# Gate slabs and output projection of the first block as unsplit float32 matmuls

## The reference

```
def mixer_ab(x, ...):
    z = rms_norm(x, norm) @ w_in
    z_gate, z_rec, z_pool = z[..., :1024], z[..., 1024:2048], z[..., 2048:]
    xr = causal_dwconv(z_rec, conv_w, conv_b)
    y_a = gelu(z_gate) * rg_lru(xr, w_gx, b_gx, w_ga, b_ga, lam)
    y_b = multi_scale_pool(z_pool, w_pool, b_pool, pool_scale)
    return concatenate([y_a, y_b], -1) @ w_out      # 1536 -> 1024
x = x + mixer_ab(x, ...)
x = x + cross_attn(x, mem, ...)                     # q from x; k, v from mem
x = x + conv_ffn(x, ...)
```

## Time and profile before

| what | value |
|---|---|
| median of 3 runs | 1840.26 us (1838.64 to 1845.79) |
| the profiled execution's own time | 1839.95 us |
| its span, first to last instruction | 1838.2 us |
| mean granted TensorE clock | 0.958 of full speed |
| busy: PE, PEld, DVE, ACT, POOL | 93%, 75%, 47%, 36%, 29% of the span |
| chain that ended last | PE 38%, issue 31%, DVE 23%, ACT 6% |

### The profile page before, as it was taken

One profiled execution on the slowest core, in us unless ns is written; L12 is line 12 of the kernel. 1 busy time (PEld: TensorE's weight loads), 2 busy tenths in 40 slices (PEclk: granted clock), 3 DMA queues, 4 the chain that ended last, 5 costly groups with the idle time before them and its releaser, 6 DMA issues.

```text
span 1838.2 us, 31174 instructions
## 1 busy us (share of the span) xinstructions
PE 1713.1 (93%) x11954; PEld 1383.8 (75%) x11954; DVE 861.1 (47%) x1409; ACT 657.1 (36%) x1127; POOL 536.1 (29%) x329
## 2 busy tenths in 40 slices
PE   7998989999999998999998999987889999989886
PEld 7887979999998797999998998877844444333333
DVE  2787447888772353588785335765411011000002
ACT  2383444444455544434433334654311111111101
POOL 0443424555467431355552443221100000000000
PEclk9999999999899989999997999998889999999997
DMA  7464523555554442355551554333779999999992
GB/s 268 153 206 152 179 92 125 185 180 177 166 167 132 161 161 82 126 186 180 174 187 40 171 185 151 101 104 125 280 307 409 409 409 409 409 410 409 409 409 91
DMA packets 108973, 398.79 MB, mean 217 GB/s; under 512 B 12097, under 2 KB 12353, under 8 KB 108481
## 3 DMA queue, kind: packets, MB, share of 16 engines
q1 hardware_dynamic: 107856, 393.26, 58.9%
q10 hardware_dynamic: 1008, 4.08, 0.6%
HBM read 396.25 MB, written 1.05 MB: 216 GB/s over the span
## 4 chain that ended last, share of the span: by engine, by line
PE 38%; issue 31%; DVE 23%; ACT 6%; POOL 1%; DVEq 1%; DMA 0%; ACTq 0%; SPq 0%; POOLq 0%
DVE wl L1154 6%; DVE cf L1455 5%; PE pw L1864 5%; PE pw L1865 5%; PE pw L1866 5%; ACT wh L636 4%; PE pw L2114 4%; DVE hid L1471 3%; PE acc L1864 3%; PE acc L1865 3%; PE acc L1866 3%; DVE cf L1458 3%; PE acc L1873 3%; PE acc L1983 2%; DVE gpad L1449 1%
## 5 line engine op out<-in xcount | busy, mean ns | idle before, releaser
L1030 POOL TENSOR_TENSOR wl<-raw,wh 128x1024 fp32r<-128x1024 f32 x165 | 402.7, 2441 | 516.0 <-ACT wh L636 515.3
L636 ACT ACTIVATE wh<-raw 128x1024 fp32r<-128x1024 f32 x330 | 342.2, 1053 | 257.6 <-PE pw L1866 151.3
L1864 PE MATMUL pw<-ah,wh 128*128 128x256 f32 x1416 | 410.2, 290 | 4.0 <-DVE gt L1604 4.0
L1865 PE MATMUL pw<-ah,wl 128*128 128x256 f32 x1416 | 406.0, 287 | 0.0
L1866 PE MATMUL pw<-al,wh 128*128 128x256 f32 x1416 | 405.7, 287 | 0.0
L1154 DVE TENSOR_TENSOR wl<-raw,wh 128x1024 fp32r<-128x1024 f32 x165 | 214.6, 1301 | 235.9 <-ACT wh L636 235.8
L1864 PEld LDWEIGHTS pw<-ah,wh 128*128 128x128 f32 x1416 | 277.6, 196 | 8.2 <-issue 6.8
L1865 PEld LDWEIGHTS pw<-ah,wl 128*128 128x128 f32 x1416 | 277.4, 196 | 0.0
L1866 PEld LDWEIGHTS pw<-al,wh 128*128 128x128 f32 x1416 | 277.2, 196 | 0.0
L1864 PE MATMUL acc<-yh,wh 128*128 128x256 f32 x832 | 245.5, 295 | 23.7 <-POOL yl L1099 5.4
L1865 PE MATMUL acc<-yh,wl 128*128 128x256 f32 x832 | 242.2, 291 | 0.0
(11 more groups left out here) (296 smaller groups left out, 2561.9 us busy)
## 6 DMA issues: line engine op xcount, KB each, us to landing
raw<-in_stream SPq DMA_DIRECT2D x506, 512.0 KB, 3.7
ring_w<-in_stream SPq DMA_DIRECT2D x96, 512.0 KB, 12.8
ring_y<-in_stream SPq DMA_DIRECT2D x72, 512.0 KB, 13.9
ring_m<-in_stream SPq DMA_DIRECT2D x48, 512.0 KB, 12.9
ring_h<-in_stream SPq DMA_DIRECT2D x24, 512.0 KB, 13.7
mem_t<-in_mem ACTq DMA_DIRECT2D x2, 1024.0 KB, 9.4
x_res<-in_x SPq DMA_DIRECT2D x2, 512.0 KB, 6.3
out<-x_res SPq DMA_DIRECT2D x1, 1024.0 KB, 3.9
```

Of the source, the lines that this page charges most:

```text
L636: A.done(act.activation(wh[:, s.base % SPLIT, :], raw[:, slot_of(s.base), :], ACT.Copy), w_hi)
L1030: G.done(pool.tensor_tensor(wl[:, s.base % SPLIT, :], raw[:, slot_of(s.base), :], wh[:, s.base % SPLIT, :].bitcast(F32), ALU.subtract), w_ ...
L1864: pe.matmul(dst, wh[:, s.base % SPLIT, w], hi, start=start, stop=False, **kw)
L1865: pe.matmul(dst, wl[:, s.base % SPLIT, w], hi, start=False, stop=False, **kw)
```

## The change

The gate slabs of `gk` and all slabs of `about` are no longer split. TensorE multiplies them as in `abin`, one float32 matmul a tile out of `raw`, with `xr` and `z` themselves as activations (`tile1`); the keys and values stay split. So the casts and subtractions into `yh` and `yl` of this block go, with their semaphores: `xr_hi`, `xr_lo`, `pooled_hi`, `pooled_lo`, `yb_hi`, `yb_lo`, `ya_hi`, `ya_lo`. In the diff, `split` is ScalarE's. Splits are numbered anew by `split_no`, and VectorE and POOL alternate by that number. The first four query slabs' splits now wait for slab s-16 instead of s-4. ScalarE waits once for all four pooled groups before the gates, since their low-part subtraction, which ordered the temporaries before, is gone. SP's loads wait for the end of an unsplit slab.

```diff
 def unsplit(s):
-    return s < S0["gk"] or S0["cw"] <= s < S0["cw"] + CW
+    if S0["gk"] <= s < S0["v0"]:
+        return (s - S0["gk"]) % 3 == 0
+    return s < S0["gk"] or S0["about"] <= s < S0["q0"] or S0["cw"] <= s < S0["cw"] + CW
...
 def split_no(s):
-    return s - S0["gk"] - (0 if s < S0["cw"] else CW)
+    if s < S0["v0"]:
+        return s - S0["gk"] - (s - S0["gk"] + 2) // 3
+    if s < S0["about"]:
+        return s - S0["gk"] - 4
+    return s - S0["gk"] - 4 - 12 - (0 if s < S0["cw"] else CW)
...
             def split(s):
...
                 if S0["v1"] <= s.base < S0["v1"] + SPLIT:
                     wait_slab(act, s + -(SPLIT + CW))
+                elif S0["q0"] <= s.base < S0["q0"] + SPLIT:
+                    wait_slab(act, s + -(SPLIT + 12))
...
+            act.wait_ge(S("pooled"), 4)
...
-                wait_emptied(act, USE0["gk"] + 5 * n + 2)
-                A.done(act.activation(yh[:, 8 + n, :], z[:, 16 + n, :], ACT.Copy), S("yb_hi"))
...
             for n in range(8):
                 if n < 7:
                     split(At(S0["v0"] + n + 1 + AHEAD))
-                act.wait_ge(S("ya_ready"), n + 1)
-                A.done(act.activation(yh[:, n, :], xr[:, n, :], ACT.Copy), S("ya_hi"))
...
-                if n:
-                    ya_lo(n - 1)
                 if n == 4:
                     v0_out(0)
-            ya_lo(7)
             v0_out(1)
...
+            def tile1(dst, s, n, src, start, stop, **kw):
+                return pe.matmul(dst, raw[:, slot_of(s.base), n * P:n * P + P], src, start=start, stop=stop, **kw)
...
-                wait_split(pe, s)
+                wait_raw(pe, s)
                 for e in range(2):
                     h = 2 * n + e
                     wait_emptied(pe, u + e - 4)
-                    pe.wait_ge(S("xr_lo"), h + 1)
+                    pe.wait_ge(S("xr_ready"), h + 1)
                     for g in range(2):
-                        last = tile3(pw[(u + e) % 4][:, g * T:g * T + T], s, 2 * e + g, yh[:, h, :], yl[:, h, :],
-                                     True, True)
+                        last = tile1(pw[(u + e) % 4][:, g * T:g * T + T], s, 2 * e + g, xr[:, h, :], True, True)
...
-            row_phase("about", [8, 9, 10, 11, 0, 1, 2, 3, 4, 5, 6, 7],
-                      lambda k: pe.wait_ge(S("yb_lo"), k - 7) if k >= 8 else pe.wait_ge(S("ya_lo"), k + 1), "mem")
+            for n in range(12):
+                s = At(S0["about"] + n)
+                wait_raw(pe, s)
+                if n < 4:
+                    wait_emptied(pe, USE0["gk"] + 5 * n + 2)
+                else:
+                    pe.wait_ge(S("ya_ready"), n - 3)
+                for c in range(KC):
+                    last = tile1(acc_of(c), s, c, z[:, 16 + n, :] if n < 4 else xr[:, n - 4, :],
+                                 n == 0 and c % 2 == 0, n == 11, skip_group_check=True)
```

More of the change, by code:

```diff
@@ L435, in wait_split @@
         def wait_split(eng, s):
-            if s.base % 2 == 0:
+            if split_no(s.base) % 2 == 0:
                 eng.wait_ge(w_lo_v, s.of(lambda n: split_no(n) // 2 + 1))
@@ L552, in _ @@
                 sp.dma_start(x[:, 4 * half:4 * half + 4, :], x_in[:, 4 * half:4 * half + 4, :]).then_inc(x_landed[half], 16)
-            for s in range(3 * RAW):
+            for s in range(6 * RAW):
                 load(At(s))
-            early, late = S0["cw"] // RAW - 2, -(-(S0["cw"] + CW) // RAW) + 1
+            early, late = S0["cw"] // RAW - 5, -(-(S0["cw"] + CW) // RAW) + 1
             with sp.Fori(0, early) as i:
                 for j in range(RAW):
-                    load(At(3 * RAW + j, RAW, i))
-            for s in range((early + 3) * RAW, late * RAW):
+                    load(At(6 * RAW + j, RAW, i))
+            for s in range((early + 6) * RAW, late * RAW):
                 load(At(s))
@@ L686, in _ @@
                                           scale=col("a_conv_w", h * CONV_A + CONV_A - 1)), S("xr_first"))
-                if n - 1 in TAP_AT:
-                    h = TAP_AT.index(n - 1)
-                    act.wait_ge(S("xr_ready"), h + 1)
-                    A.done(act.activation(yh[:, h, :], xr[:, h, :], ACT.Copy), S("xr_hi"))
                 if 8 <= n < 12:
@@ L693, in _ @@
                     mem_hi(0, 2 * n - 15)
-                if n in (9, 12, 15, 18):
-                    g = n // 3 - 3
-                    act.wait_ge(S("pooled"), g + 1)
-                    A.done(act.activation(yh[:, 8 + g, :], z[:, 16 + g, :], ACT.Copy), S("pooled_hi"))
                 if n >= 14:
@@ L1065, in _ @@
                     G.done(pool.tensor_tensor(z[:, 16 + g, :], src, z[:, 16 + g, :], ALU.subtract), S("pooled"))
-                if n in (10, 13, 16, 19):
-                    g = (n - 10) // 3
-                    pool.wait_ge(S("pooled_hi"), g + 1)
-                    G.done(pool.tensor_tensor(yl[:, 8 + g, :], z[:, 16 + g, :], yh[:, 8 + g, :].bitcast(F32),
-                                              ALU.subtract), S("pooled_lo"))
             splits(S0["gk"], 12)
@@ L1274, in xr_taps @@
                                                     ALU.mult, ALU.add), S("xr_ready") if k == CONV_A - 1 else None)
-            def xr_lo(h):
-                dve.wait_ge(S("xr_hi"), h + 1)
-                V.done(dve.tensor_tensor(yl[:, h, :], xr[:, h, :], yh[:, h, :].bitcast(F32), ALU.subtract),
-                       S("xr_lo"))
             def slab_out(s, u, dst):
@@ L1335, in _ @@
                 split(At(gate_slab(n) + AHEAD))
-                if n == 0:
-                    xr_lo(7)
                 u = USE0["gk"] + 5 * n
@@ L2146, in _ @@
             pe.wait_ge(S("v0_out"), TT)
-            row_phase("about", [8, 9, 10, 11, 0, 1, 2, 3, 4, 5, 6, 7],
-                      lambda k: pe.wait_ge(S("yb_lo"), k - 7) if k >= 8 else pe.wait_ge(S("ya_lo"), k + 1), "mem")
+            for n in range(12):
[8 more added lines that the diff above has]
+                                 n == 0 and c % 2 == 0, n == 11, skip_group_check=True)
+                    if n == 11 and c < KC - 1:
+                        last.then_inc(acc_full, 1)
+                last.then_inc(slab_done, 1)
             def spread_hook(name):
```

18 lines of the change are left out of this document (4 added, 14 removed).

## The result

The changed kernel takes **1824.0 us**, median of 5 runs (1816.49 to 1827.48), against 1839.43 us of the kernel before in the same comparison (5 runs, 1834.89 to 1845.79): ratio 0.9914, 95% interval 0.9886 to 0.9942. That is faster by 15.4 us and by more than 0.5%. Its profiled execution took 1825.4 us with a span of 1823.6, against 1839.95 and 1838.2. The prediction was 1831.1 us with a range from 1827.0; the measured time lies 3.0 us under the range.

A forecast was written before the change was run, and what follows sets the result against it. TensorE, busy 93% of the span, was taken as the bound. Gate/key -2.3, value stage -3.7, output projection -0.2 and junction -2.7 gave -8.9 us from 1839.95, so 1831.1 us, range 1827.0 to 1837.0.

The forecast's parts named there:

- The price of a tile: TensorE's 116 unsplit tiles: each goes from 0.36 to 0.433 us, +8.5 us, all on the path.
- rival of dearer tiles: Unsplit float32 tiles cost 0.48 us here instead of 0.433, 5.4 us more, total 1836.5; chance 0.07.
- Open weight loads: Unsplit tiles: each float32 record waits for its weight load, 43 us more, net 1865; chance 0.04.
- Gate/key: Gate and key slabs: TensorE sets the pace, most waits go, 1.3 us stay; values start at 125.2, -2.3 us.
- Value stage: Value slabs before the output projection: idle time for the v_m copy goes, 26.0 to 22.0 us, 0.3 given back, -3.7.
- the tie: End of value stage: v_m copies done at 147.0, matmuls at 147.2, so no more than a few tenths idle.
- Output projection: Twelve unsplit slabs take 41.6 us, about as long as before; dearer matmuls offset lost waits and low clock, -0.2 us.
- Junction: Projection's end to first query matmul: sums start earlier, queries 4.0 us behind instead of 6.7, one half-clock stretch kept, -2.7 us.
- rival with all waits gone: Gate/key and junction: removed waits go altogether and junction keeps full clock, -12.1 us, total 1827.9; chance 0.23.
- All later stages follow the same chain and shift with it: Everything behind the first query matmul: only starts earlier, with no gain or loss of its own.
- At nothing: Weight stream, SP's queue order, masks' transfer, pooled-groups wait and POOL's work: counted as costing or saving nothing.
- the sum: Total over the three stages and the junction: -2.3, -3.7, -0.2 and -2.7 make -8.9 us, giving 1831.1.

The follow-up runs named there:

- middle_split: Changed kernel with output-projection slabs 44 to 47 split again, casts and subtractions for heads 0 to 3 placed behind splits and v_m copies: 1820.34 us, ratio 0.9891.
- prologue_only: Kernel before with only SP's loads of slabs 36 to 71 written out instead of looped, all slabs split as before: 1832.87 us, ratio 0.9954.
- gates_unsplit_casts_behind: Changed kernel with output projection split, y_a casts behind value splits, subtractions behind v_m copies, first v_m copy one head earlier: 1832.14 us, ratio 0.9952 to kernel before.
- again: The changed kernel unaltered, timed against the kernel before in more rounds: 1824.67 us, ratio 0.9898.
- longer_prologue: Changed kernel with twelve more of SP's loads (slabs 72 to 83) written out: 1819.99 us, ratio 0.9888 to the kernel before.

## Why the prediction was wrong, and where it was right

**The price of a tile: right.** 96 tiles of the projection took 41.54 us without idle time, 0.433 us each, as in the first projection. The rival of dearer tiles, and the rule of the Trainium skill beside it (FP8 and Floating Point Precision, "TensorE Precision Notes"), would have given 0.48 and 46.1 us for the stage; 0.433 is 3.6 times the 0.12 us of a split matmul. That speaks against the price that I made of the rule, not against four passes, which no run here counts. middle_split shows the price once more from the other side: 32 tiles back to three matmuls took 2.3 us off, 0.073 a tile. Open weight loads, the rival on the slower side, did not occur: weight loads were 36.56 us of work beside 41.50 of matmuls.

**Gate/key: the number right in part by luck.** 32.75 us against 33.0. The waits that remained are 0.31 and 0.26 us at the keys' copy, where I had 1.3 together; VectorE is held there by POOL, but catches up sooner. TensorE itself was busy for 32.2 us, where I had 31.7: two small errors that nearly cancel.

**Value stage: right**, the tie too. I had the copies of v_m at 147.0 with values from 125.2, which is 21.8 us into the stage. They start at 149.36 and last 1.28, so end 21.8 us in, 0.06 before the projection's first matmul. Two of VectorE's operations were held, as I had it, the scan of 136.20 for 2.77 us and this one, with the POOL split beside it, VectorE first:

```profile
142.38 2.44 DVE L1338 TENSOR_TENSOR xr<-xr,z 128x256 f32<-128x256 f32 x1
...
149.36 1.28 DVE L1305 COPY v_m<-acc 128x512 f32<-128x512 f32 x2
```

```profile
141.18 3.35 POOL L1027 TENSOR_TENSOR wl<-raw,wh 128x1024 fp32r<-128x1024 f32 x1 [2.76 <-ACT wh L644]
```

The operation of 0.42 us ends 0.3 us behind the POOL split. The Trainium skill, SBUF — State Buffer, "SBUF: two separate sides", has VectorE and GpSimd share one port pair under an exclusive lock; the held operation agrees with it.

**Output projection: right**, 41.5 us for 41.6, and clock 1.00 throughout.

**Junction: right.** The sums start 2.4 us before the last product, as forecast, and the queries 3.95 behind it. VectorE's and ScalarE's timelines:

```profile
189.85 3.35 DVE L1191 TENSOR_TENSOR x_res<-acc,x_res 128x256 f32<-128x256 f32 x8 [22.93 <-PE acc L1841]
```

```profile
190.31 0.42 ACT L650 ACTIVATE sq<-x_res 128x256 f32<-128x256 f32 x1 [24.65 <-DVE x_res L1191]
```

The stretch at the low level behind it stayed, 0.56 over 3.9 us, where the rival with all waits gone had full clock. So that rival was false here, and in gate/key, where about half of the waits that it removes did go, the stage came nearer to the forecast's 33.0 than to its 31.7.

One sum of the rivals is wrong: open weight loads at 43 us would have made 1874 and not 1865. It carries no bound of the range.

**What failed is the sentence "All later stages follow the same chain and shift with it"**, and with it the part *At nothing*. I had gone through SP's queue for its order and its waits, not for its code. The whole diff has 36 more written-out loads on SP. Neither the cuts of it shown above nor the prediction name them, and the sum has them at nothing without a reason. The transfers are the same; the code that SP fetches is not. Their price is -6.4 us in the profiled executions and -7.4 in the runs of prologue_only. With it the sum is -8.9-6.4 = -15.3 us, 1824.7, and the measured time 1824.0. The range failed by the same omission: its ends were worked out from the three stages alone, and no rival touched anything behind them. The page of the kernel before had the signs: GB/s of 409 or 410 in the nine slices from 1379 to 1792 us, so a stage bound by transfers, and 41 packets of q14, of which I did not ask when they came.

Of the chances, faster had 0.47 and no difference 0.49. That the change came out clearly faster is owed to a share that I had not seen: the head's 9.4 us alone would have been at the border of what a measurement tells.

## What to carry to other kernels

Cost the code of a loop as well as its work: writing out loads, or a loop, on one engine changes what that engine fetches later, and in a stage where the weight stream has no slack, code that is fetched anew in every trip can cost nearly as much as a whole round of tuning wins (here 7 us, beside 9.4 in the head). Look at when the instruction packets come, and whether they repeat with a loop's period. An engine that does more passes can still win where it frees the two that feed it: measure the price of an unsplit tile against the waits that the split brings, and keep the split where the feeding engines have time, as in the middle of the projection.

## What the runs showed of the hardware that was not expected

- In a weight stream at 409 GB/s, ten more instruction packets of 8 KB within the expert stage (15 against 5) cost it 6.8 us (before against prologue_only), in steps of mostly 0.7, with the mean DMA share unchanged and 30 of the 32 parts of a slab pair on time. Of 14 profiled executions, those with 40 or 41 packets had a stage of 466.6 or 466.7 us, those with 30 or 32 one of 459.3 to 460.5.
- Whether the loop is fetched anew is all or nothing over the lengths of the code in front that were tried: 0 and 12 loads more had the fetches, 36 had not, nor had 48 in the changed kernel. Where the border lies, and whether there is more than one, was not tried.
- Two engines' operations in each other's way are not a fixed price. In gates_unsplit_casts_behind VectorE made four subtractions in 1.42 us, and four like them in 5.74 beside POOL's splits.
- Six runs of the changed kernel, again and longer_prologue take 1815.4 to 1816.5 us at a granted clock of 0.966 or 0.967, where the others take 1822 to 1827.5 at 0.958 to 0.962. Left open: which stretches of lower clock they were spared, and why. No profiled execution was among them.
